# Latent attention on one core: the residual turned before it is scaled, wider compressed projections, four banks for the fills, and the keys squared on GpSimd

## The chip, the cores and the metric

One core of one Trainium2 chip runs the whole program. The metric is the device time of one execution in microseconds (us), as the median of several runs. Lower is better. All of the times below are of this core. The engines are named as in the profile: PE is TensorE's matmul side and PEld its weight load, DVE is VectorE, ACT is ScalarE, POOL is GpSimd, SP is SyncE, which issues most DMAs.

## What is computed

Two blocks of a transformer run on a sequence of 512 positions with a residual of 1024 columns. The first block has a gated mixer and dilated attention and a feed-forward layer with a norm behind it. The second block has two layers: layer 0 mixes with latent attention (the stage of this study) and layer 1 with an mLSTM, each followed by a feed-forward layer with a squared ReLU. The part that matters, from the reference:

```python
def mla_mixer(h, w_dq, q_norm, w_uq, w_dkv, kv_norm, w_ukv, q_gain, k_gain, w_o):
    b, s, _ = h.shape
    pos = jnp.arange(s)
    cq = rms_norm_2(h @ w_dq, q_norm)
    q = (cq @ w_uq).reshape(b, s, MLA_HEADS, MLA_QK)
    dkv = h @ w_dkv
    ckv = rms_norm_2(dkv[..., :MLA_KV_RANK], kv_norm)
    k_rope = jnp.broadcast_to(dkv[..., None, MLA_KV_RANK:], (b, s, MLA_HEADS, MLA_ROPE))
    kv = (ckv @ w_ukv).reshape(b, s, MLA_HEADS, MLA_NOPE + MLA_V)
    k = jnp.concatenate([kv[..., :MLA_NOPE], k_rope], axis=-1)
    v = kv[..., MLA_NOPE:]
    q = rms_norm_2(q, q_gain)
    k = rms_norm_2(k, k_gain)
    ...
```

Here `h` is the residual x after `rms_norm_2(x, norm_mix[0])`, which is x divided by the root of its mean square plus 1e-6, times a gain for each column. The query rank is 384, the key and value rank 256, the shared rotary part 32 columns; there are 16 heads of 96 (64 plus 32 rotary) with values of 64.

## The kernel before

Every float32 product is made as three matmuls of a reduced float32 form (`mm3`, L82 to L84): each operand is split into a high part and the rest, the low part. ScalarE makes the high part of a unit of weights (`split_hi`, L320), VectorE subtracts it to get the low part (`split_lo`, L326). Weights come in units of at most 2048 columns of the buffers `raw_weights`, `weights_hi` and `weights_lo`, which hold two units each; `plan_units` lists them in the order of use, and SyncE loads them in that order (`load_unit`, L312). A split may overwrite the unit two before it once `release` says that enough groups of matmuls have ended; `held` adds groups of the next unit to that number.

Each engine runs its own list of instructions in the order written; semaphores tie them together. A function such as `ffn`, `mla_down` or `mla` writes the lists for one stage.

**The hand-over.** The feed-forward layer of the first block (`ffn`) ends with a norm over its output, and adds it to the residual X (`updated`, L1592), first for the row tiles 0 and 1, then for 2 and 3. The next norm (`norm_halves`, here with `whole=True`) goes by the same halves. ScalarE sums the squares of each tile (`last_sum`, L392) and takes the root (L397); VectorE inverts the roots and scales the rows into a buffer XN (`normed`, L432 and L436; ScalarE scales tile 3, `normed_last`, L441); TensorE transposes XN (`turned`, L451) into PSUM; ScalarE makes the high part with the gain (`hi`, L461), VectorE the low part (`lo`, L493). GpSimd takes part of the multiplications by the gain in the norm behind the feed-forward layer (L1350).

**The compressed projections** (`mla_down`). The first unit has 256 of the 384 query columns, the second the other 128 and the 32 shared rotary columns, the third the 256 key and value columns. For each row tile, TensorE runs `first` (8 steps of k, 256 columns) and `second` (8 steps, 160 columns) into one bank, tiles 0 and 1 before tiles 2 and 3, with the turning of the second half between them. Then come the key and value columns, four tiles. Each result is squared and summed on ScalarE (L1723, L1712) and normed on VectorE (L1744 to L1762).

**Latent attention** (`mla`). The 16 heads are in four groups g of four. For each group, TensorE fills queries (`q`, 384 columns) and keys with values (`kv`, 512 columns) for each of 4 row tiles; ScalarE empties each bank (`empty`, L1952 to L1965). The jobs take the banks 5 and 7 in turn, and a job waits until the one before it in its bank is emptied. ScalarE squares the queries and the keys of a group into one buffer SQ (`squares`, L1975), VectorE sums them (`sums`, L2054), rotates (`rotate`, L2074 to L2077) and scales the keys (`norm`). Groups 0 and 1 are filled ahead of the heads, groups 2 and 3 among them. For each head n: scores (L1889), mask and maximum on VectorE (`mask`, L2086, and `shift`, L2093), exponentials on ScalarE (L1986), transposes of the probabilities in three parts (`turn`, L1899), copies to SBUF (parts 0 and 2 on ScalarE, L2032; part 1 on VectorE, L2153), values (L1911). The weights of later groups are split between heads, as `SPLITS` says: head 1 splits unit 4, which is the third query unit.

## Time and profile before

| What | Before |
|---|---|
| median of 3 runs | 2036.82 us (2035.33 to 2037.03) |
| the profiled execution | 2034.55 us |
| its span, first to last instruction | 2032.8 us |
| PE busy | 2010.8 us (99%) |
| DVE, ACT, POOL busy | 942.5, 844.7, 22.0 us |
| hand-over and compressed projections | about 837 to 887 us of the span |
| latent attention | about 887 to 1060 us |

An instruction's row in the timeline has its start, its duration, engine and line, what it writes and reads, and the count where neighbours of a kind are merged. What stands in brackets at the end is the time for which the engine was idle before it, and what ended that. Matmuls are pipelined, so the duration of one is longer than the distance between two starts; the distance is what a stream of them costs. Line numbers are those of the kernel before.

### The profile page before, as it was taken

The numbers are of one execution on the slowest core, as the hardware profiler recorded it, in microseconds if no ns is written. First come the engines' busy times: TensorE is split into PE (matmuls) and PEld (weight loads), VectorE is DVE, ScalarE is ACT, GpSimd is POOL, SyncE is SP. The second block draws the span as 40 slices with busy tenths as digits, with TensorE's granted clock in tenths as the row PEclk, the third lists the DMA queues.
The fourth block names the chain that finished last, engine by engine and source line by source line (L and its number), as shares of the span: only waits on it lengthen the run. The fifth ranks groups of instructions, "written<-read, shape, count | busy, mean of one in ns | idle before, by whom it ended". The sixth has DMA issues, their size and how long they took to land.

```text
span 2032.8 us, 24823 instructions
## 1 busy us (share of the span) xinstructions
PE 2010.8 (99%) x10074; PEld 1699.7 (84%) x10074; DVE 942.5 (46%) x1328; ACT 844.7 (42%) x1181; POOL 22.0 (1%) x38
## 2 busy tenths in 40 slices
PE   8999999999999999999999999999999999999999
PEld 7888888888888888887889888888888789888887
DVE  5654553345434343656745443434433455343443
ACT  5333324225433333558854433333464544333332
POOL 1000000000000000010000000000000000000000
PEclk9999999999999999999999999999999999999999
DMA  7232222332233323211012332232222123323322
GB/s 235 80 86 73 78 75 67 102 114 94 86 101 103 99 87 103 66 57 44 21 43 84 104 103 96 89 103 86 81 83 82 64 63 103 104 83 103 100 91 81
DMA packets 162880, 178.84 MB, mean 88 GB/s; under 512 B 7001, under 2 KB 125358, under 8 KB 162674
## 3 DMA queue, kind: packets, MB, share of 16 engines
q1 hardware_dynamic: 161762, 176.62, 27.4%
q8 instruction: 57, 0.93, 0.2%
q0 software_dynamic: 1024, 1.12, 0.2%
q14 instruction: 21, 0.17, 0.0%
q10 hardware_dynamic: 16, 0.00, 0.0%
HBM read 174.51 MB, written 2.10 MB: 87 GB/s over the span
## 4 chain that ended last, share of the span: by engine, by line
PE 93%; DVE 4%; ACT 2%; issue 0%; DMA 0%; SPq 0%; DVEq 0%; ACTq 0%
PE psum L82 28%; PE psum L83 28%; PE psum L84 28%; PE psum L1911 1%; PE psum L1889 1%; DVE weights_lo L326 1%; PE psum L842 1%; PE psum L2325 1%; PE psum L820 1%; PE psum L1899 1%; PE psum L451 1%; PE psum L1867 0%; PE psum L2308 0%; PE psum L828 0%; ACT weights_hi L320 0%
## 5 line engine op out<-in xcount | busy, mean ns | idle before, releaser
L82 PE MATMUL psum<-norm_T_hi,weights_hi 128*128 128x512 f32 (+1 forms) x1440 | 538.6, 374 | 0.7 <-DVE norm_T_lo L493 0.5
L84 PE MATMUL psum<-norm_T_hi,weights_lo 128*128 128x512 f32 (+1 forms) x1440 | 533.5, 370 | 0.0
L83 PE MATMUL psum<-norm_T_lo,weights_hi 128*128 128x512 f32 (+1 forms) x1440 | 533.1, 370 | 0.0
L82 PE MATMUL psum<-weights_hi,act_T_hi 128*128 128x512 f32 (+1 forms) x912 | 354.1, 388 | 2.3 <-DVE weights_lo L326 1.0
L84 PE MATMUL psum<-weights_hi,act_T_lo 128*128 128x512 f32 (+1 forms) x912 | 352.4, 386 | 0.0
L83 PE MATMUL psum<-weights_lo,act_T_hi 128*128 128x512 f32 (+1 forms) x912 | 352.3, 386 | 0.0
L1432 ACT ACTIVATE weights_hi<-raw_weights 128x2048 fp32r<-128x2048 f32 x92 | 175.7, 1910 | 343.7 <-PE psum L84 343.7
L82 PEld LDWEIGHTS psum<-norm_T_hi,weights_hi 128*128 128x128 f32 x1440 | 271.3, 188 | 46.8 <-DVE norm_T_lo L493 0.8
L84 PEld LDWEIGHTS psum<-norm_T_hi,weights_lo 128*128 128x128 f32 x1440 | 271.2, 188 | 46.6
L83 PEld LDWEIGHTS psum<-norm_T_lo,weights_hi 128*128 128x128 f32 x1440 | 271.5, 189 | 45.2
L1529 DVE TENSOR_TENSOR weights_lo<-raw_weights,weights_hi 128x2048 fp32r<-128x2048 f32 x92 | 210.9, 2292 | 110.4 <-ACT weights_hi L1432 110.4
L326 DVE TENSOR_TENSOR weights_lo<-raw_weights,weights_hi 128x2048 fp32r<-128x2048 f32 (+3 forms) x74 | 157.1, 2123 | 167.9 <-ACT weights_hi L320 167.9
L1537 DVE TENSOR_TENSOR act_T_lo<-scratch,act_T_hi 128x512 fp32r<-128x512 f32 x96 | 66.6, 694 | 318.3 <-ACT act_T_hi L1443 318.3
L82 PEld LDWEIGHTS psum<-weights_hi,act_T_hi 128*128 128x128 f32 x912 | 171.2, 188 | 37.6 <-issue 1.4
L84 PEld LDWEIGHTS psum<-weights_hi,act_T_lo 128*128 128x128 f32 x912 | 171.2, 188 | 33.6
L83 PEld LDWEIGHTS psum<-weights_lo,act_T_hi 128*128 128x128 f32 x912 | 171.3, 188 | 33.2
L1439 ACT ACTIVATE scratch<-psum 128x512 f32<-128x512 f32 x96 | 57.3, 597 | 273.5 <-PE psum L84 273.5
L320 ACT ACTIVATE weights_hi<-raw_weights 128x2048 fp32r<-128x2048 f32 (+3 forms) x74 | 130.9, 1769 | 71.7 <-PE psum L84 71.7
L82 PE MATMUL psum<-weights_hi,norm_T_hi 128*128 128x512 f32 (+3 forms) x384 | 134.7, 351 | 1.1 <-DVE norm_T_lo L493 0.9
L83 PE MATMUL psum<-weights_lo,norm_T_hi 128*128 128x512 f32 (+3 forms) x384 | 132.3, 345 | 0.0
L84 PE MATMUL psum<-weights_hi,norm_T_lo 128*128 128x512 f32 (+3 forms) x384 | 132.2, 344 | 0.0
L1546 DVE TENSOR_TENSOR residual<-psum,residual 128x512 f32<-128x512 f32 x112 | 76.5, 691 | 103.3 <-PE psum L84 103.3
(266 smaller groups left out, 1816.7 us busy)
## 6 DMA issues: line engine op xcount, KB each, us to landing
raw_weights<-in_ffn_w_dram SPq DMA_DIRECT2D x64, 1024.0 KB, 5.2
raw_weights<-in_w_up_dram SPq DMA_DIRECT2D x16, 1024.0 KB, 5.3
raw_weights<-in_w_down_dram SPq DMA_DIRECT2D x16, 1024.0 KB, 5.1
raw_weights<-in_w_in_dram SPq DMA_DIRECT2D x26, 512.0 KB, 5.1
raw_weights<-in_w_in_dram SPq DMA_DIRECT2D x11, 1024.0 KB, 5.2
raw_weights<-in_mlstm_w_in_dram SPq DMA_DIRECT2D x8, 1024.0 KB, 5.1
raw_weights<-in_w_in_dram SPq DMA_DIRECT2D x24, 256.0 KB, 3.4
raw_weights<-in_w_out_dram SPq DMA_DIRECT2D x4, 1024.0 KB, 5.1
```

The lines of the kernel that those rows point to most:

```text
L82: pe.matmul(out, ah, bh, start=start, stop=False)
L83: pe.matmul(out, ah, bl, start=False, stop=False)
L84: return pe.matmul(out, al, bh, start=False, stop=stop)
L320: act.activation(WH[:, u % 2, 0:c], RAW[:, u % 2, 0:c], ACT.Copy).then_inc(w_hi, 1)
L326: dve.tensor_tensor(WL[:, u % 2, 0:c], RAW[:, u % 2, 0:c], WH[:, u % 2, 0:c].bitcast(F32), SUB).then_inc(w_lo, 1)
L451: mm = pe.transpose(PS[:, bank, q * P:q * P + P], XN[:, t, k * P:k * P + P], IDENT[:, :])
L820: mm = pe.matmul(at_bank, QK[:, h % 2, g, 0, t * P:t * P + P], QK[:, h % 2, g, 1, lo * P:hi * P], start=True, stop=True)
L1432: act.activation(WH[:, u % 2, :], RAW[:, u % 2, :], ACT.Copy).then_inc(w_hi, 1)
L1439: act.activation(HS[:, f, :], PS[:, up_banks[f], :], ACT.Relu).then_inc(fr.sem, 1)
L1529: dve.tensor_tensor(WL[:, u % 2, :], RAW[:, u % 2, :], WH[:, u % 2, :].bitcast(F32), SUB).then_inc(w_lo, 1)
L1537: dve.tensor_tensor(AL[:, f, :], HS[:, f, :], AH[:, f, :].bitcast(F32), SUB).then_inc(fl.sem, 1)
L1546: dve.tensor_tensor(z, PS[:, banks[t], :], z, ADD).then_inc(acc.sem, 1)
```

## The change

Five things change, all in this part of the program.

1. `norm_halves` gets a form `behind=True`, used for the norm ahead of latent attention. TensorE turns X itself, as soon as its tiles are updated. The rows aren't scaled. The sums of squares (`row_sum`), roots and factors are made later. The compressed query and key norms take the missing factor into account: with r the mean square plus 1e-6 of a row, the epsilon inside their mean becomes r times 1e-6, and the common factor cancels. The shared rotary columns are multiplied by the factor when they are copied.
2. The first two units are cut along k instead of along columns: each has four steps of k with all 416 columns (384 query and 32 rotary), so that one matmul covers 416 columns.
3. The jobs up to the first heads (the first 20) go over four banks, 5, 7, 4 and 6.
4. GpSimd squares the keys of groups 1 to 3.
5. Unit 4 is split ahead of the heads (on ScalarE behind the first key tile of group 1, on VectorE ahead of the first mask), and VectorE sums and rotates group 1's queries ahead of the first mask.

```diff
-    add(4, dq[:, :, 0:256], held=2)
-    add(4, dq[:, :, 256:384], dkv[:, :, 256:288], side=True)
+    for i in range(2):
+        add(4, dq[:, 4 * i:4 * i + 4, :], dkv[:, 4 * i:4 * i + 4, 256:288], side=True, held=0 if i else 2)
...
                 def turned(pe, h):
-                    pe.wait_ge(xnc.sem, xnc.at(3 if whole and h else 2 * h + 2))
-                    if whole and h:
-                        pe.wait_ge(xlc.sem, xlc.at(1))
+                    if behind:
+                        pe.wait_ge(updated.sem, updated.at(2 * h + 2))
+                    else:
+                        pe.wait_ge(xnc.sem, xnc.at(3 if whole and h else 2 * h + 2))
+                        if whole and h:
+                            pe.wait_ge(xlc.sem, xlc.at(1))
...
# ffn, ScalarE
-                    for t in (0, 1):
-                        act.wait_ge(res.sem, res.at(t + 1))
-                        nxt.last_sum(act, t)
                     split_hi(act, u0 + 4 * NF)
# ffn, VectorE
                     updated(0)
-                    nxt.normed(dve, 0)
                     add(0, 2)
...
# mla_down, TensorE
+                def rows(i, t, ready=None):
+                    tt = slice(t * P, t * P + P)
+                    for k in range(4 * i, 4 * i + 4):
+                        if ready:
+                            ready(pe, k)
+                        w = slice(416 * (k % 4), 416 * (k % 4) + 416)
+                        mm = mm3(pe, PS[:, banks[t], 0:416], NTH[:, k, tt], NTL[:, k, tt],
+                                 WH[:, (u0 + i) % 2, w], WL[:, (u0 + i) % 2, w], k == 0, k == KD - 1)
+                    mm.then_inc(gemm, 1)
                 pe.wait_ge(w_lo, u0 + 1)
-                first(0)
-                first(1)
+                rows(0, 0, norm.ready(0))
+                rows(0, 1)
                 pe.wait_ge(w_lo, u0 + 2)
-                second(0)
-                second(1)
+                rows(1, 0, norm.ready(0))
+                rows(1, 1)
                 norm.turned(pe, 1)
-                first(2)
-                first(3)
-                second(2)
-                second(3)
+                rows(0, 2, norm.ready(1))
+                rows(0, 3)
+                rows(1, 2, norm.ready(1))
+                rows(1, 3)
# mla_down, ScalarE
+                for t in (0, 1):
+                    norm.row_sum(act, t)
+                norm.hi(act, 1)
                 for t in (2, 3):
                     act.wait_ge(res_in.sem, res_in.at(t + 1))
-                    norm.last_sum(act, t)
-                norm.normed_last(act)
-                norm.hi(act, 1)
+                    norm.row_sum(act, t)
+                norm.row_roots(act)
                 split_hi(act, u0 + 2)
# mla_down, VectorE
-                norm.normed(dve, 1)
                 norm.lo(dve, 1)
+                norm.row_means(dve)
+                norm.row_factors(dve)
                 split_lo(dve, u0 + 2)
                 dve.wait_ge(sq.sem, sq.at(4))
-                dve.tensor_scalar(m0[:, 0:4], s0[:, 0:4], 1.0 / QR, EPS, MUL, ADD).then_inc(ms.sem, 1)
+                dve.wait_ge(norm.means_made.sem, norm.means_made.at(2))
+                dve.wait_ge(norm.factor_made.sem, norm.factor_made.at(1))
+                dve.scalar_tensor_tensor(m0[:, 0:4], s0[:, 0:4], 1.0 / QR, norm.eps, MUL, ADD).then_inc(ms.sem, 1)
...
-                    dve.tensor_copy(KRR[:, t, :], PS[:, banks[t], QR:QR + MROPE]).then_inc(kr_c.sem, 1)
+                    dve.tensor_scalar(KRR[:, t, :], PS[:, banks[t], QR:QR + MROPE], norm.factor[:, t:t + 1], None, MUL).then_inc(kr_c.sem, 1)
...
# mla
             def bank(m):
-                return 5 if m % 2 == 0 else 7
-            SPLITS = {1: 4, 2: 5, 3: 6, 5: 7, 10: 8, 13: 9}
+                return (5, 7, 4, 6)[m % 4] if m < 20 else (5, 7)[m % 2]
+            SPLITS = {2: 5, 3: 6, 5: 7, 10: 8, 13: 9}
...
# mla, ScalarE
                 for t in range(NT):
                     empty(("kv", 1, t))
+                    if t == 0:
+                        split_hi(act, u0 + 4)
...
-                    if n % 4 == 0 and g < 4:
-                        squares(g, 1)
# mla, GpSimd
+            @block.gpsimd
+            def _(pool):
+                for g in range(1, 4):
+                    pool.wait_ge(xn.sem, xn.at(g + 1))
+                    pool.wait_ge(ms.sem, ms.at(3 * g + 1))
+                    pool.wait_ge(ev.sem, ev.at(emptied[idx[("kv", g, NT - 1)]]))
+                    k = QKB[:, g % 2, 1536:3072]
+                    pool.tensor_tensor(SQ, k, k, MUL).then_inc(sq.sem, 1)
# mla, VectorE
                 norm(0)
+                sums(1, 0)
+                rotate(1, 0)
+                split_lo(dve, u0 + 4)
                 mask(0, 3)
                 shift(0, slice(3, 4))
                 masks(0)
-                sums(1, 0)
-                rotate(1, 0)
...
-            after = norm_halves(C_N0, *turn[1], halves, whole=True)
+            after = norm_halves(C_N0, *turn[1], halves, behind=True)
```

The new steps of the norm:

```python
def row_sum(act, t):
    act.activation(XN[:, t, :], X[:, t, :], ACT.Square, accum_out=s1[:, t:t + 1]).then_inc(s1c.sem, 1)
def row_roots(act):
    act.wait_ge(m0c.sem, m0c.at(1))
    act.activation(root, m0, ACT.Sqrt).then_inc(rtc.sem, 1)
def row_means(dve):
    dve.wait_ge(s1c.sem, s1c.at(NT))
    dve.tensor_scalar(m0, s1, 1.0 / D, EPS, MUL, ADD).then_inc(m0c.sem, 1)
    dve.wait_ge(m0c.sem, m0c.at(1))
    dve.tensor_scalar(s0, m0, EPS, None, MUL).then_inc(m0c.sem, 1)
def row_factors(dve):
    dve.wait_ge(rtc.sem, rtc.at(1))
    dve.reciprocal(rstd, root).then_inc(rsc.sem, 1)
```

## Rows read from the trace of the kernel before

**Rows 1.** Windows: busy time (count) of PE, PEld, DVE, ACT, POOL; granted clock; DMA.

```profile
600.00:800.00 200.00, 200.00 (x885) 165.58 (x884) 79.72 (x75) 66.86 (x72) 0.00 (x0) 1.00 0.31 100
...
924.00:936.00 12.00, 10.09 (x72) 8.80 (x73) 11.69 (x36) 11.41 (x19) 0.00 (x0) 1.00 0.00 1
```

**Rows 2.** Waits of TensorE, 840 to 1030 us: total, times, longest.

```profile
PE psum L82 <- ACT scratch L1952: 0.7, 2, 0.4
...
PE psum L82 <- ACT scratch L1958: 0.6, 1, 0.6
```

**Rows 3.** Timeline of TensorE, 842 to 863 us, the hand-over.

```profile
842.99 1.97 PE L451 MATMUL psum<-ident,scratch 128*128 128x128 f32 x16 [1.13 <-DVE scratch L436]
...
848.03 0.36 PE L82 MATMUL psum<-weights_hi,norm_T_hi 128*128 128x256 f32 x1 [0.35 <-DVE norm_T_lo L493]
...
860.26 1.94 PE L451 MATMUL psum<-ident,scratch 128*128 128x128 f32 x16 [0.78 <-ACT scratch L441]
...
862.73 0.39 PE L82 MATMUL psum<-weights_hi,norm_T_hi 128*128 128x256 f32 x1 [0.53 <-DVE norm_T_lo L493]
```

**Rows 4.** Timeline of TensorE, 924 to 936 us, the first heads.

```profile
924.25 0.41 PE L1899 MATMUL psum<-ident,scratch 128*128 128x128 f32 x2 [0.88 <-ACT scratch L2032]
...
931.64 0.41 PE L1899 MATMUL psum<-ident,scratch 128*128 128x128 f32 x2 [0.49 <-ACT scratch L2032]
...
935.28 0.41 PE L82 MATMUL psum<-weights_hi,act_T_hi 128*128 128x384 f32 x1 [1.03 <-DVE weights_lo L326]
```

**Rows 5.** Timeline of TensorE: starts of one kind, of 256, 160 and 384 columns.

```profile
852.91 0.28 PE L82 MATMUL psum<-weights_hi,norm_T_hi 128*128 128x256 f32 x1
...
853.63 0.28 PE L82 MATMUL psum<-weights_hi,norm_T_hi 128*128 128x256 f32 x1
...
855.63 0.27 PE L82 MATMUL psum<-weights_hi,norm_T_hi 128*128 128x160 f32 x1
...
856.30 0.28 PE L82 MATMUL psum<-weights_hi,norm_T_hi 128*128 128x160 f32 x1
...
892.36 0.33 PE L82 MATMUL psum<-weights_hi,act_T_hi 128*128 128x384 f32 x1
...
892.88 0.33 PE L82 MATMUL psum<-weights_hi,act_T_hi 128*128 128x384 f32 x1
```

**Rows 6.** Timeline of VectorE and ScalarE, 837 to 873 us.

```profile
837.11 2.48 DVE L1592 SCALAR_TENSOR_TENSOR residual<-scratch,small,residual 128x1024 f32<-128x1024 f32 x2
...
851.63 1.28 DVE L1575 TENSOR_TENSOR scratch<-psum,scratch 128x512 f32<-128x512 f32 x2
...
854.57 2.48 DVE L1592 SCALAR_TENSOR_TENSOR residual<-scratch,small,residual 128x1024 f32<-128x1024 f32 x2
...
869.04 1.92 ACT L320 ACTIVATE weights_hi<-raw_weights 128x2048 fp32r<-128x2048 f32 x1 [5.09 <-PE psum L84]
...
870.99 2.29 DVE L326 TENSOR_TENSOR weights_lo<-raw_weights,weights_hi 128x2048 fp32r<-128x2048 f32 x1 [5.96 <-ACT weights_hi L320]
```

**Rows 7.** Timeline of VectorE: the split beside GpSimd's multiplications.

```profile
844.04 3.06 DVE L326 TENSOR_TENSOR weights_lo<-raw_weights,weights_hi 128x2048 fp32r<-128x2048 f32 x1
```

**Rows 8.** Timeline of VectorE and ScalarE, 918 to 964 us.

```profile
918.20 0.69 DVE L2086 CUSTOM_DVE_ANT_0 scratch<-psum,chunk_masks 128x512 f32<-128x512 f32 x1 [7.86 <-PE psum L1889]
...
920.30 1.75 DVE L2054 TENSOR_REDUCE small<-scratch 128x16 f32<-128x1536 f32 x1
...
924.09 0.68 DVE L2086 CUSTOM_DVE_ANT_0 scratch<-psum,chunk_masks 128x512 f32<-128x512 f32 x1
...
961.28 1.48 ACT L1975 ACTIVATE scratch<-scratch 128x1536 f32<-128x1536 f32 x1
...
963.11 0.60 ACT L2032 ACTIVATE scratch<-psum 128x512 f32<-128x512 f32 x1 [0.34 <-PE psum L1899]
...
963.95 0.16 DVE L2093 SCALAR_TENSOR_TENSOR small<-small 128x1 f32<-128x1 f32 x1
```

**Rows 9.** Source line L1350: ns minimum, median, maximum; first and last start us.

```profile
L1350 POOL TENSOR_TENSOR scratch<-scratch x2: 1271/2302/3332, 843.7 to 844.9; 128x512 f32<-128x512 f32 x2
```

More of the change, by code:

```diff
@@ L370, in in_order, with norm_halves @@
             return x.rearrange("p (i r) -> p r i", r=NT)
-        def norm_halves(which, banks_a, banks_b, part, whole=False, apart=False):
+        def norm_halves(which, banks_a, banks_b, part, whole=False, apart=False, behind=False):
             XN = SCR[:, 0:NT * D].rearrange("p (t d) -> p t d", t=NT)
@@ L377, in norm_halves @@
             marks = {}
-            for c, n in ((n_s0, 0 if whole or apart else NT), (n_s1, 3 if apart else NT), (n_sv, 1 if apart else 0), (n_m0, 0 if whole or apart else 2),
-                         (n_rt, 3 if apart else NT), (n_rs, 3 if apart else 2), (n_xn, 3 if whole else NT), (n_xl, 1 if whole else 0), (n_tp, 8), (n_th, 2 * KD), (n_tl, 2 * KD)):
+            updated = resid.copy()
+            for c, n in ((n_s0, 0 if whole or apart or behind else NT), (n_s1, 3 if apart else NT), (n_sv, 1 if apart else 0), (n_m0, 2 if behind else 0 if whole or apart else 2),
+                         (n_rt, 1 if behind else 3 if apart else NT), (n_rs, 1 if behind else 3 if apart else 2), (n_xn, 0 if behind else 3 if whole else NT), (n_xl, 1 if whole else 0), (n_tp, 8), (n_th, 2 * KD), (n_tl, 2 * KD)):
                 marks[c] = c.copy()
@@ L450, in turned @@
                             k, t = 2 * b + q // 2, 2 * h + q % 2
-                            mm = pe.transpose(PS[:, bank, q * P:q * P + P], XN[:, t, k * P:k * P + P], IDENT[:, :])
+                            mm = pe.transpose(PS[:, bank, q * P:q * P + P], (X if behind else XN)[:, t, k * P:k * P + P], IDENT[:, :])
                         mm.then_inc(tpc.sem, 1)
@@ L502, in ready @@
                     return wait
+            Steps.eps, Steps.factor, Steps.means_made, Steps.factor_made = s0, rstd, m0c, rsc
             return Steps
@@ L1678, in _ @@
             def _(pe):
-                def first(t):
-                    group_N(pe, u0, 0, 256, 256, KD, PS[:, banks[t], 0:256], t, NTH, NTL,
-                            ready=None if t % 2 else norm.ready(t // 2))
-                def second(t):
-                    group_N(pe, u0 + 1, 0, 160, 160, KD, PS[:, banks[t], 256:416], t, NTH, NTL)
+                def rows(i, t, ready=None):
[7 more added lines that the diff above has]
+                    mm.then_inc(gemm, 1)
                 pe.wait_ge(w_lo, u0 + 1)
-                first(0)
-                first(1)
+                rows(0, 0, norm.ready(0))
+                rows(0, 1)
                 pe.wait_ge(w_lo, u0 + 2)
-                second(0)
-                second(1)
+                rows(1, 0, norm.ready(0))
+                rows(1, 1)
                 norm.turned(pe, 1)
-                first(2)
-                first(3)
-                second(2)
-                second(3)
+                rows(0, 2, norm.ready(1))
+                rows(0, 3)
+                rows(1, 2, norm.ready(1))
+                rows(1, 3)
                 pe.wait_ge(w_lo, u0 + 3)
@@ L1756, in _ @@
                 dve.wait_ge(sq.sem, sq.at(8))
-                dve.tensor_scalar(m0[:, 4:8], s0[:, 4:8], 1.0 / KVR, EPS, MUL, ADD).then_inc(ms.sem, 1)
+                dve.scalar_tensor_tensor(m0[:, 4:8], s0[:, 4:8], 1.0 / KVR, norm.eps, MUL, ADD).then_inc(ms.sem, 1)
                 dve.wait_ge(rt.sem, rt.at(2))
@@ L1845, in job @@
                     m = idx[what]
-                    if m >= 2:
-                        pe.wait_ge(ev.sem, ev.at(emptied[m - 2]))
-                        if order[m - 2][0] == "out":
-                            pe.wait_ge(tl.sem, tl.at(order[m - 2][1] + 1))
+                    same = [i for i in range(m) if bank(i) == bank(m)]
+                    if same:
+                        last = same[-1]
+                        pe.wait_ge(ev.sem, ev.at(emptied[last]))
+                        if order[last][0] == "out":
+                            pe.wait_ge(tl.sem, tl.at(order[last][1] + 1))
                     kind = what[0]
```

5 lines of the change are left out of this document (added).

## The prediction

> **What bounds the kernel now.** I read the windows first, because a share of busy time over the whole span hides where the losses lie. In a stretch of feed-forward work TensorE has no idle time, 200.00 of 200.00 us; from 924 to 936 us it was busy for 10.09 of 12.00 us, while VectorE was busy for 11.69 and ScalarE for 11.41 [rows 1]. So TensorE sets the end nearly everywhere, and a stage is worth changing in two ways only: its idle time, or its own work. The profile's engine shares (the table above) say the same: 99% for TensorE, so all its idle time together is 22 us.
>
> Next the waits of TensorE between 840 and 1030 us: a few tenths each, for instance 0.7 us in two waits on the copies that empty the query products and 0.6 us in one on those of the keys and values [rows 2]. Then the timeline of TensorE. In the hand-over from the feed-forward layer to the compressed projections it idles 1.13 and 0.35 us around the first turning of the residual, 0.78 and 0.53 us around the second [rows 3]. Among the heads of latent attention it idles 0.88 and 0.49 us for the ScalarE copy on L2032 and 1.03 us for the low part of weights [rows 4]. The clock column shows full speed (1.00, the 2.4 GHz level) in both windows [rows 1]; nothing here changes what precedes it, so it stays out of the sum.
>
> **Part 1: 416 columns in one matmul.** Before, each of 4 row tiles took 8 x 3 products of 256 columns and 8 x 3 of 160: 96 of each. After, 96 of 416. Starts of the same kind six matmuls apart (three for 384 columns) give the pitch: 256 columns (853.63 - 852.91) / 6 = 0.120 us; 160 columns (856.30 - 855.63) / 6 = 0.112 us; 384 columns (892.88 - 892.36) / 3 = 0.173 us [rows 5]. The 160-column matmul costs almost what the 256-column one does: there is a floor. From 256 to 384 columns the slope is 0.053 / 128, so 416 columns should take 0.173 + 32 x 0.00042 = 0.187 us. Saving: 96 x (0.120 + 0.112 - 0.187) = 4.3 us, all of it on TensorE's own path. Bounds: no less than the 384-column pitch (saving 5.6), no more than that of 512 columns, 200 / 885 = 0.226 us [rows 1] (saving 0.6). I take 0.187, since 416 lies next to 384.
>
> The Trainium skill (TensorE: Matmul & The Clock Gate, section Back-to-back issue gap) gives N / 2.4 + 2.5 ns for an isolated matmul. By it 256 and 160 columns cost 109 + 69 ns and 416 costs 176 ns, so joining them saves an estimated 0.2 us in all: it speaks against this part, and would put the whole change at 3.7 us instead of 7.8. The trace disagrees with it, with 112 ns at 160 columns [rows 5].
>
> **Part 2: the residual turned unscaled, first half.** The turning waited for the sum of squares, the root, the reciprocal and the scaling. Now it waits only for the update of the residual, which ended at 837.11 + 2.48 = 839.6 us [rows 6], before TensorE was free at 842.99 - 1.13 = 841.9 [rows 3]. The 1.13 us go. The 0.35 us behind them came from VectorE reaching the low parts late (848.03): it stood behind the scaling and behind one weight split that took 3.06 us [rows 7]. The scaling leaves this queue and the split covers 1664 columns instead of 2048, so it goes too. With the restart of the pipe (0.1 to 0.2 us each) I take 1.7 us; bounds 1.1 and 1.8.
>
> **Part 3: the second half.** TensorE reaches it after 48 wide matmuls: 848.03 - 1.7 + 48 x 0.187 = 855.3 us. Before, the update ended 5.4 us after VectorE's additions of 851.63 (854.57 + 2.48 = 857.05) [rows 6]. These stand behind the second weight split, and all of that chain moves up by what the first half gained, about 1.7 us, less 0.4 us because the second split grows from 1280 to 1664 columns and plus 0.2 us that its ScalarE part waited. Additions at 850.1, update ended at 855.5, turning at 855.6: 0.3 us idle instead of 0.78. The 0.53 us from the turning to the first product stay, as that is ScalarE and VectorE making the first high and low parts. After it VectorE delivers a pair of tiles each 0.8 us, and TensorE now needs 6 x 0.187 = 1.1 us for a pair, so the small pacing losses that the second half showed (some 0.3 us) go. I take 0.8 us; bounds 0 and 1.2. The sums of squares move to ScalarE's spare time behind the high parts; their factors are wanted only by the norms of the compressed tiles, later.
>
> What becomes late next is the third unit's split. It can start when two of the four second-half groups are done: before at 869.04, low part ready at 870.99 + 2.29 = 873.3 [rows 6], and TensorE came 1.1 us later. Now half of the remaining work is 24 x 0.187 = 4.5 us, while high and low parts take 1.9 + 2.3 us and the hand-overs: they meet within 0.1 us. I charge nothing and keep 0.5 us for the range. The new multiplications by the factor replace instructions of the same size; the unit loads have the same total bytes and are issued earlier. Sum for the projections: 4.3 + 1.7 + 0.8 = 6.8 us.
>
> **Part 4: four banks and the moved split.** From here VectorE is nearly the path: it is busy nearly without a pause from 924 to 936 us [rows 1], but it idled 7.86 us before the first mask at 918.20 [rows 8]. The four banks let TensorE run further ahead in the fills, so their waits [rows 2], some 2 us with restarts, go, and the first scores are there near 914.5. In its freed time, from 918.20 - 7.86 = 910.3, VectorE now does the sums and rotation of group 1's queries (920.30 to 924.09, 3.8 us) [rows 8] and the split that TensorE waited for (1152 columns, by 2.29 us for 2048 some 1.4 us) [rows 6]. If nothing else came, the first mask would be at 910.3 + 3.8 + 1.4 = 915.5 instead of 918.2. The transposes followed it by 924.25 - 918.20 = 6.05 us, 0.88 of it for ScalarE's square [rows 4], which leaves; I keep 0.8 us for ScalarE's other copies, which then press, and get 921.5 instead of 924.25. The waits of 0.49 and 1.03 us, with their restarts 1.85 us, also go: ScalarE no longer splits that unit between heads, and its low part is made. Gain 2.75 + 1.85 = 4.6 us.
>
> **Part 5: GpSimd squares the keys.** A multiply of 128x512 on GpSimd took between 1.27 and 3.33 us [rows 9]; in the same stretch VectorE's weight split lasted 3.06 us instead of 2.29 [rows 6, 7]. I read this as turns: VectorE stood until the first multiply ended, GpSimd stood until the split ended. The square has 1536 columns: 3 x 1.27 = 3.8 us if it has its turn; 3 x 3.33 = 10 us is the other bound. I assume that VectorE instructions that read PSUM are free of it, as only the split was long, and that every one with two SBUF operands is not. The Trainium skill (GPSIMD Engine Reference, Specifications) says the SBUF interfaces are shared with VectorE, with contention for instructions with two SBUF inputs. The trace agrees, with 3.06 against 2.29 us.
>
> Group 1: the square can start when group 1's keys are out and its query sums are read, about 912.7, in the middle of the rotation and ahead of the split. If VectorE stands 3.8 us there, the first mask comes at 919.3 and the transposes at 919.3 + 6.05 - 0.88 = 924.5: part 4's 2.75 us are lost and 1.6 us remain. If VectorE keeps the port until the split is done, only its small shift instruction waits, and some 3.2 us remain. Groups 2 and 3: the square starts where ScalarE's did, 961.28, and ends at about 965.1. In it falls the shift at 963.95, a two-SBUF operation: it waits some 1 us, and the copy behind it, which TensorE waits for, too. ScalarE gains nothing there, for it sat idle 0.34 us after its square anyway [rows 8]. I take 0.7 us lost in each; bounds 0 and 1.1. Sum for attention: 2.4 (midway between 1.6 and 3.2, as no row says who has the turn) - 1.4 = 1.0 us.
>
> **The number.** 6.8 + 1.0 = 7.8 us. The profiled execution took 2034.55 us (span 2032.8), 2.3 us under the median of 2036.82; I set the gain against its own terms, giving 2026.7, and against the median 2029.0 us.
>
> **Rivals.**
> (a) GpSimd is in nobody's way: VectorE's long split was long for another reason. For it: the two durations on GpSimd differ by a factor of 2.6, a sign that one is odd. Against it: the times fit turns. Gain 6.8 + 4.6 = 11.4: 2025.4 us.
> (b) The wide matmul costs the sum of the narrow ones: gain 7.8 - 4.3 = 3.5 us, 2033.3 us. The rows at 160 and 384 columns speak against it. This is where the rule named in part 1 would lead.
> (c) The third unit's weights come late: nearer 2 us than 0.1 us, from ScalarE still at sums and root when the split is due. 2030.9 us. Against it: those end a microsecond before it.
> (d) The change does not do what it says at the hand-over: the update of the residual, not the norm, is last, and the idle times stay. Gain 7.8 - 2.5 = 5.3: 2031.5 us. For it: in the second half the update is indeed within 0.3 us of last.
> (e) Slower. Each square takes the 10 us of the second multiply and VectorE's two-operand work stands for it. Group 1 loses 6.2 us more; in groups 2 and 3 the sums, due at 966.7, come at 971.3, 4.6 us each. 6.8 + 1.6 - 6.2 - 9.2 = -7.0 us: 2043.8 us. Beyond 5.4 us all three squares count, and it decides from about 7.7 us a square: (d - 3.8) + 2 x (d - 5.4) = 8.4.
>
> **Chances.** Forecast 0.55, (a) 0.22, (b) 0.06, (c) 0.07, (d) 0.05, (e) 0.05. A measurement of this kernel tells about 0.2%, 4.1 us, from no change. Faster: forecast, (a), (c), (d), 0.89; within it (b), 0.06; slower (e), 0.05. Range: below, (a) with its own microsecond of scatter, 2024.0; above, the forecast with part 1 at 0.2 us and 1.1 us lost per square, through (c) and (d), 2032.5.
>
> **What would show it.** 96 matmuls of 128x416 at a pitch near 0.187 us; no idle time before the first transposes of L451 and 0.2 to 0.4 us before the second; squares on GpSimd of 3.8 us; in the same stretch a rotation or split on VectorE two or three times its usual length; shifts of 1 us in groups 2 and 3; no wait on low weights at the second query group. Wrong would be a pitch over 0.2 us, a square over 7 us, or a new wait on low weights before the third unit.

## The result, and the profile after

The changed kernel takes 2026.03 us (median of 4 runs, 2024.82 to 2027.68), the kernel before 2036.74 us (4 runs, 2035.33 to 2037.03). The ratio is 0.995, with a 95% interval of 0.9938 to 0.9962: 10.7 us faster. The profiled execution after took 2025.99 us (span 2024.2), against 2034.55 us before: 8.6 us between the two traces. The 2.1 us between these two gains go with the granted clock of the runs of before, which is taken up below. The four runs of the changed kernel differ in it too: the one with a mean clock of 1.000 took 2024.82 us, two with 0.999 took 2025.99 and 2026.07, and one with 0.998 took 2027.68.

The page's line of engines after:

```profile
PE 2006.0 (99%) x9978; PEld 1695.8 (84%) x9978; DVE 943.2 (47%) x1326; ACT 837.4 (41%) x1174; POOL 30.5 (2%) x41
```

TensorE's busy time fell by only 4.8 us (2010.8 to 2006.0), so about half of the gain is idle time. The waits of TensorE after, 836 to 1030 us (line waited on, total, times, longest):

```profile
PE psum L1925 <- DVE small L2131: 2.2, 1, 2.2
PE psum L82 <- DVE norm_T_lo L521: 0.5, 1, 0.5
PE psum L1947 <- DVE scratch L2199: 0.4, 1, 0.4
PE psum L1935 <- ACT scratch L2068: 0.4, 2, 0.2
```

The waits on ScalarE in the fills [rows 2] and the one on the low weights [rows 4] are gone, of those on ScalarE's copies among the heads 0.4 us are left, and one new wait of 2.2 us has come: the scores of the second head, on the masks that VectorE makes of the first (L2131).

**The projections.** TensorE after, from the turning of the residual (L479) through the compression (416 columns) to the first query product (384 columns):

```profile
841.81 0.40 PE L84 MATMUL psum<-weights_hi,act_T_lo 128*128 128x512 f32 x1
842.04 1.91 PE L479 MATMUL psum<-ident,residual 128*128 128x128 f32 x16
843.71 0.47 PE L82 MATMUL psum<-weights_hi,act_T_hi 128*128 128x512 f32 x1
...
850.49 0.36 PE L82 MATMUL psum<-weights_hi,norm_T_hi 128*128 128x416 f32 x1
...
851.62 0.36 PE L82 MATMUL psum<-weights_hi,norm_T_hi 128*128 128x416 f32 x1
...
855.38 0.34 PE L84 MATMUL psum<-weights_hi,norm_T_lo 128*128 128x416 f32 x1
855.73 1.97 PE L479 MATMUL psum<-ident,residual 128*128 128x128 f32 x16
858.22 0.46 PE L82 MATMUL psum<-weights_hi,norm_T_hi 128*128 128x416 f32 x1 [0.53 <-DVE norm_T_lo L521]
...
880.34 0.34 PE L82 MATMUL psum<-weights_hi,act_T_hi 128*128 128x384 f32 x1
```

The turnings carry no bracket any more, where before they stood behind 1.13 and 0.78 us of idle time [rows 3]. The second starts 0.35 us after the last matmul where the pitch is 0.19: 0.16 us lost. The 0.53 us behind it stayed. Six wide matmuls take 851.62 - 850.49 = 1.13 us: a pitch of 0.188 us. The first query product starts at 880.34 instead of 886.95, 6.61 us earlier; the last product of the feed-forward layer started 0.34 us later than before (841.81, against 841.47 in the trace of before), so the projections themselves gained 6.95 us.

**The first heads.** TensorE after. L1925 makes scores, L1935 turns the masked scores, L1947 multiplies them with the values, and the last line is the second group's first query product:

```profile
911.97 3.79 PE L1925 MATMUL psum<-key_rows,scratch 96*128 96x512 f32 x8 [2.25 <-DVE small L2131]
915.56 0.92 PE L1935 MATMUL psum<-ident,scratch 128*128 128x128 f32 x4
916.32 0.60 PE L1903 MATMUL psum<-ident,scratch 128*96 128x128 f32 x4
...
917.63 0.38 PE L1935 MATMUL psum<-ident,scratch 128*128 128x128 f32 x2
...
920.03 2.38 PE L1925 MATMUL psum<-key_rows,scratch 96*128 96x512 f32 x8
...
926.60 0.42 PE L82 MATMUL psum<-weights_hi,act_T_hi 128*128 128x384 f32 x1
```

The last line answers to 935.28 [rows 4]: 8.68 us earlier, of which 6.61 were already there, so the attention added 2.07 us. Behind the wait of 2.25 us the same eight score matmuls took 3.79 us, and 2.38 us one head later. The windows (length, busy time and count of TensorE, granted clock, DMA share, GB/s) say why:

```profile
908.00:910.00 2.00, 1.72 (x7) 1.00 0.00 0
910.00:912.00 2.00, 0.03 (x1) 1.00 0.00 0
912.00:914.00 2.00, 2.00 (x4) 0.70 0.50 163
914.00:916.00 2.00, 2.00 (x8) 0.50 0.38 140
916.00:918.00 2.00, 2.00 (x19) 0.95 0.00 0
```

The granted clock fell to 0.50, the 1.2 GHz level, right behind the idle time, and was back at 2.4 GHz some 4 us later. It cost 3.79 - 2.38 = 1.4 us in the scores, and some 0.3 us more in the four transposes behind them, which took 916.32 - 915.56 = 0.76 us from start to start (0.44 in e5 below). VectorE in the same stretch, with the rotation (L2119 to L2122), the split (L327), the first mask (L2131) and the shift (L2138):

```profile
905.43 1.29 DVE L2119 TENSOR_TENSOR scratch<-scratch 128x512 f32<-128x512 f32 x2
906.76 2.85 DVE L2121 TENSOR_TENSOR scratch<-scratch 128x256 f32<-128x256 f32 x1
909.54 0.41 DVE L2122 TENSOR_TENSOR scratch<-scratch 128x256 f32<-128x256 f32 x1
909.87 1.34 DVE L327 TENSOR_TENSOR weights_lo<-raw_weights,weights_hi 128x1152 fp32r<-128x1152 f32 x1
911.14 0.68 DVE L2131 CUSTOM_DVE_ANT_0 scratch<-psum,chunk_masks 128x512 f32<-128x512 f32 x1
```

And GpSimd's three squares (L2088):

```profile
906.28 3.05 POOL L2088 TENSOR_TENSOR scratch<-scratch 128x1536 f32<-128x1536 f32 x1 [22.45 <-ACT scratch L1994]
952.69 2.75 POOL L2088 TENSOR_TENSOR scratch<-scratch 128x1536 f32<-128x1536 f32 x1 [43.35 <-ACT scratch L1994]
991.37 2.75 POOL L2088 TENSOR_TENSOR scratch<-scratch 128x1536 f32<-128x1536 f32 x1 [35.93 <-ACT scratch L1994]
```

The rotation of 256 columns took 2.85 us where its twin took 0.41: it ended 0.3 us after the first square did (906.28 + 3.05 = 909.33). VectorE stood for 2.4 us, the first mask was made that much later, and TensorE ran dry.

### The profile page after: what moved, and what is told of

Read it like the earlier page. It is cut to its first block, busy times and chain, and to the rows that moved or that the text cites. A ratio compares the mean times of both kernels' runs of the same rounds, so it can differ in the third digit from the quotient of the medians.

```text
span 2024.2 us, 24613 instructions
## 1 busy us (share of the span) xinstructions
PE 2006.0 (99%) x9978; PEld 1695.8 (84%) x9978; DVE 943.2 (47%) x1326; ACT 837.4 (41%) x1174; POOL 30.5 (2%) x41
## 4 chain that ended last, share of the span: by engine, by line
PE 94%; DVE 3%; ACT 1%; DMA 0%; issue 0%; SPq 0%; ACTq 0%; DVEq 0%
PE psum L82 28%; PE psum L84 28%; PE psum L83 28%; PE psum L1947 2%; PE psum L1925 2%; PE psum L871 1%; PE psum L2371 1%; PE psum L849 1%; PE psum L1935 1%; PE psum L479 1%; DVE weights_lo L327 1%; PE psum L1903 1%; PE psum L2354 0%; PE psum L857 0%; ACT weights_hi L321 0%; DMA raw_weights<-in_w_in_dram 0%
## 5 line engine op out<-in xcount | busy, mean ns | idle before, releaser
L327 DVE TENSOR_TENSOR weights_lo<-raw_weights,weights_hi 128x2048 fp32r<-128x2048 f32 (+3 forms) x74 | 156.9, 2121 | 166.7 <-ACT weights_hi L321 166.6
L82 PE MATMUL psum<-weights_hi,norm_T_hi 128*128 128x512 f32 (+3 forms) x352 | 127.6, 362 | 1.1 <-DVE norm_T_lo L521 0.5
L84 PE MATMUL psum<-weights_hi,norm_T_lo 128*128 128x512 f32 (+3 forms) x352 | 125.5, 357 | 0.0
L83 PE MATMUL psum<-weights_lo,norm_T_hi 128*128 128x512 f32 (+3 forms) x352 | 125.4, 356 | 0.0
```

What stands on the lines that cost most here:

```text
L82: pe.matmul(out, ah, bh, start=start, stop=False)
L83: pe.matmul(out, ah, bl, start=False, stop=False)
L84: return pe.matmul(out, al, bh, start=False, stop=stop)
L327: dve.tensor_tensor(WL[:, u % 2, 0:c], RAW[:, u % 2, 0:c], WH[:, u % 2, 0:c].bitcast(F32), SUB).then_inc(w_lo, 1)
```

## The experiments

Each kernel ran on one of three chips, beside runs of the kernel before on the same chip; their medians there were 2035.08 (e1 to e4), 2036.78 (e5 to e8) and 2036.88 us (e9, e10), of 19, 9 and 9 runs. The chips themselves are alike: the runs of before with a mean clock of 1.000 took 2034.79 to 2035.31, 2034.97, and 2034.80 and 2034.85 us on them. Edits are against the changed kernel where nothing else is said.

**e1: narrow units again.** The compression has units of 256 and 160 columns and its loops as before; the norm and the attention stay as changed.

```
-    for i in range(2):
-        add(4, dq[:, 4 * i:4 * i + 4, :], dkv[:, 4 * i:4 * i + 4, 256:288], side=True, held=0 if i else 2)
+    add(4, dq[:, :, 0:256], held=2)
+    add(4, dq[:, :, 256:384], dkv[:, :, 256:288], side=True)
...
```

> The changed kernel with the units of before: 256 and 160 columns in two matmuls instead of 416 in one. Theory: the pitch decides, 96 x (0.120 + 0.112 - 0.187) = 4.3 us come back; about 0.3 us of it may be hidden, since the update of the residual is no longer waited for in the second half. Span about 2028.2 instead of 2024.2 us. Rival: streaming of columns alone sets the cost (0.2 us by the rule named in the prediction), and the gain at the projections came from the earlier turning; then the span stays within 0.5 us of 2024.2.

Measured: 2029.84 us (ratio 0.9973, 0.9962 to 0.9983), span 2027.9, 3.7 us over that of the changed kernel, and the first query product at 884.08, 3.74 us later. The wide rows are worth 3.7 us behind the new norm, where 4.3 less some 0.3 were expected, and the wait of 2.2 us before the scores is there as well.

**e2: the norm as before, wide rows kept.** The residual is scaled before it is turned.

```
-                halves, behind=True)
+                halves, whole=True)
...
                     updated(0)
+                    nxt.normed(dve, 0)
```

> The changed kernel with the norm of before at the hand-over (rows scaled ahead of the turning), wide matmuls and the new attention kept. Theory: TensorE idles again about 1.1 and 0.35 us around the first turning, and around the second more than the 0.78 us of before, since the wide matmuls bring it there 2.2 us earlier while the chain sum of squares, root, scaling still takes 3.2 us behind the update: some 3.3 us idle in place of 0.2. Span about 2024.2 + 1.7 + 3.1 = 2029 us. Rival: each part stands alone, and undoing this one costs the 2.5 us that the prediction gave it: 2026.7 us.

Measured: 2031.38 us (ratio 0.9979, 0.997 to 0.9988), span 2030.1: 5.9 us over, where 4.8 were expected and 2.5 by the rival. The second turning in it, and TensorE's windows there:

```profile
860.84 3.24 PE L479 MATMUL psum<-ident,scratch 128*128 128x128 f32 x16 [3.31 <-ACT scratch L466]
863.74 0.70 PE L82 MATMUL psum<-weights_hi,norm_T_hi 128*128 128x416 f32 x1
```

```profile
860.00:862.00 2.00, 1.16 (x8) 0.82 0.00 0
862.00:864.00 2.00, 2.00 (x11) 0.50 0.00 0
864.00:866.00 2.00, 2.00 (x11) 0.82 0.00 0
```

The wait was 0.78 us [rows 3] and is 3.31 us: the wide rows bring TensorE to the second half sooner, and the scaled tiles come no sooner. Then the clock falls, and from the first transpose to the next product are 863.74 - 860.84 = 2.90 us instead of 843.71 - 842.04 = 1.67. These 1.2 us are about what the expectation lacked. The time from the last product of the feed-forward layer to the first query product gives all four pairings of norm and rows:

| Norm | Rows | from, to | us |
|---|---|---|---|
| old | narrow (before) | 841.47, 886.95 | 45.48 |
| old | wide (e2) | 842.06, 886.29 | 44.23 |
| new | narrow (e1) | 841.58, 884.08 | 42.50 |
| new | wide (the change) | 841.81, 880.34 | 38.53 |

With the old norm the wide rows are worth 1.25 us and with the new one 3.97: with the old one, most of what they save goes into a wait that is 2.5 us longer and into the fall of the clock behind it. So the two parts can't be priced apart and added (3.7 + 5.9 is more than the 6.95 us of both).

**e3: the attention as before.** Two banks, the old split, the squares on ScalarE; the function of the latent attention is that of before, all else is the changed kernel. The core of the edit:

```
-                return (5, 7, 4, 6)[m % 4] if m < 20 else (5, 7)[m % 2]
+                return 5 if m % 2 == 0 else 7
-            SPLITS = {2: 5, 3: 6, 5: 7, 10: 8, 13: 9}
+            SPLITS = {1: 4, 2: 5, 3: 6, 5: 7, 10: 8, 13: 9}
...
+                    if n % 4 == 0 and g < 4:
+                        squares(g, 1)
```

> The changed kernel with the whole attention stage of before (two banks, keys squared by ScalarE, unit 4 split at head 1), new hand-over and projections kept. Theory: the stage gained 2.1 us in the trace (935.28 to 926.60 is 8.7 us, 6.6 of them already there at its first query product), so the span is about 2026.3 us. Rival: the stage's gain is only the position of one trace, and the span stays within 0.5 us of 2024.2.

Measured: 2029.37 us (ratio 0.9968, 0.9955 to 0.998), span 2027.5: 3.3 us over, 1.2 more than expected. The expectation set a trace with a fall of the clock (the change) against one without (before); here both have one. At a mean clock of 1.000 the difference is the same: 2028.0 us in two runs against 2024.8 in one. TensorE has its old waits back, and the clock falls behind the last of them (the columns as above):

```profile
917.39 0.41 PE L1932 MATMUL psum<-ident,scratch 128*128 128x128 f32 x2 [0.88 <-ACT scratch L2065]
924.79 0.41 PE L1932 MATMUL psum<-ident,scratch 128*128 128x128 f32 x2 [0.50 <-ACT scratch L2065]
928.43 0.54 PE L82 MATMUL psum<-weights_hi,act_T_hi 128*128 128x384 f32 x1 [1.03 <-DVE weights_lo L327]
```

```profile
928.00:930.00 2.00, 1.57 (x5) 0.64 0.20 27
930.00:932.00 2.00, 2.00 (x8) 0.51 0.72 268
```

These are the waits of [rows 4], and in the trace of before the clock stayed at 1.00 behind them. So the same three waits are followed by a fall in one execution and by none in another; two of the six runs of e3 have a mean clock of 1.000. What decides it, no run here shows.

**e4: the first square later.** GpSimd squares the second group's keys only when the first head's masks are made.

```
                 for g in range(1, 4):
+                    if g == 1:
+                        pool.wait_ge(smk.sem, smk.at(4))
                     pool.wait_ge(xn.sem, xn.at(g + 1))
```

> The changed kernel, in which GpSimd's first square waits until VectorE has made the masks of head 0, when VectorE idles 3.4 us. Theory (turns on the SBUF port): the rotation instruction that took 2.85 us takes 0.42 again, the first mask comes 2.4 us earlier, TensorE's 2.25 us wait for it goes, and the span falls by some 2.3 us to about 2021.9. Rival 1: the rotation was long for a reason of its own, and nothing changes. Rival 2: the wait goes to another link (exponentials, or the copies on ScalarE) and less than 1 us is gained.

Measured: 2021.80 us (2021.67 to 2022.06, 5 runs; ratio 0.9932, 0.9918 to 0.9945), span 2020.1: 4.1 us less than the changed kernel, where 2.3 were expected, and the clock is at 1.0 in every run. VectorE and GpSimd in it:

```profile
906.75 0.42 DVE L2123 TENSOR_TENSOR scratch<-scratch 128x256 f32<-128x256 f32 x1
...
908.70 0.68 DVE L2133 CUSTOM_DVE_ANT_0 scratch<-psum,chunk_masks 128x512 f32<-128x512 f32 x1
```

```profile
910.71 2.74 POOL L2090 TENSOR_TENSOR scratch<-scratch 128x1536 f32<-128x1536 f32 x1 [26.87 <-DVE small L2133]
```

The square lasts 2.74 us, as in the other groups, but lies where VectorE is idle or reads PSUM, but for a shift of one column just ahead of its end (913.25, 0.21 us for 0.16). The rotation is back at 0.42 us, the first mask comes 2.44 us earlier, and neither the wait nor the fall of the clock is there. This is the fastest kernel of the study, faster than both given ones.

**e5: TensorE kept busy in the wait.** Nine matmuls of 512 columns into a bank that is free at that time, ahead of the second head's scores; their product is thrown away.

```
+                        if n == 1 and i == 0:
+                            for r in range(9):
+                                pe.matmul(PS[:, 7, :], AH[:, r % 3, 0:P], AL[:, r % 3, :], start=True, stop=True)
                         if n and c == 0:
                             pe.wait_ge(smk.sem, smk.at(4 * n - 4 + (1, 3, 4)[b]))
```

> The changed kernel with nine matmuls of 512 columns, whose result nobody reads, put where TensorE waits 2.25 us for the first mask. The wait itself stays. Theory: the wait costs twice, once as idle time and once because the granted clock falls to 0.5 behind it (the scores at 911.97 took 3.79 us instead of 2.38). With TensorE busy the clock stays at 1.00 and the span falls by 1.4 us to about 2022.8, and the spread of the runs shrinks. Rival: the fall has nothing to do with the idle time; then the span stays at 2024.2 or grows by what the nine matmuls overlap.

Measured: 2024.32 us (2024.12 to 2024.86, 5 runs; ratio 0.994, 0.9926 to 0.9953), span 2022.5: 1.7 us less by doing more.

```profile
909.55 2.41 PE L1925 MATMUL psum<-act_T_lo,act_T_hi 128*128 128x512 f32 x9
912.01 2.45 PE L1928 MATMUL psum<-key_rows,scratch 96*128 96x512 f32 x8
914.30 0.60 PE L1938 MATMUL psum<-ident,scratch 128*128 128x128 f32 x4
914.74 0.60 PE L1903 MATMUL psum<-ident,scratch 128*96 128x128 f32 x4
```

The scores start where they did (912.01 against 911.97) and take 2.45 us instead of 3.79. So the 1.4 us are the clock's and not the scores' own. The four transposes behind them are back at 0.44 us from start to start, and the second group's query product starts at 925.02 for 926.60: the fall cost 1.6 us in all, which is what the span shows (1.7). The DMA traffic behind the wait isn't the cause: from 912 to 916 us the DMA share in e5 is 0.47 and 0.39, as in the change (0.50 and 0.38), at a clock of 1.00. All five runs have a mean clock of 1.000. Of the twelve runs of the change and of e1, whose traces have the same wait, three do: the idle time makes the fall likely, and not certain.

**e6: the squares by ScalarE.** The changed kernel with GpSimd's block taken out and ScalarE squaring the keys between heads, as before; four banks and the moved split stay.

```
                         split_hi(act, u0 + SPLITS[n])
+                    if n % 4 == 0 and g < 4:
+                        squares(g, 1)
```

> The changed kernel without GpSimd's squares: ScalarE squares the keys of groups 1 to 3 as before. Theory: the long rotation is gone as in the late-square kernel, so most of its 4.1 us are gained too; ScalarE's 1.48 us ahead of the copies of head 0 cost up to 1 us of it: span 2020.1 to 2021.1. In groups 2 and 3 nothing changes. Rival: GpSimd's squares are what relieves ScalarE, and without them all heads at 0, 4 and 8 lose about 1 us each: 2023 us.

Measured: 2022.54 us (2022.45 to 2022.72; ratio 0.9931, 0.9917 to 0.9944), span 2020.7. That is 3.5 us less than the changed kernel and 0.6 us more than e4, as expected. GpSimd's help, as placed in the change, costs 3.5 us; placed as in e4 it is worth 0.6 us. The difference to e4 lies in this wait of e6, which is 0.4 us there:

```profile
PE psum L1935 <- ACT scratch L2070: 1.2, 3, 0.7
```

**e7: two banks.** The late square of e4, with two banks for the fills.

```
-                return (5, 7, 4, 6)[m % 4] if m < 20 else (5, 7)[m % 2]
+                return (5, 7)[m % 2]
```

> The late-square kernel (span 2020.1) with the fills back in two banks. Theory: the fills end later, about where they did in the kernel with the attention of before (first scores near 910.3 instead of 907.3 us), so the first mask comes some 2.3 us later: span about 2022.4. Rival: VectorE's chain sets the first mask with either number of banks, and the four banks are worth less than 0.5 us.

Measured: 2025.24 us (ratio 0.9944, 0.993 to 0.9958), span 2023.2: 3.1 us over e4, where 2.3 were expected. The first mask is at 911.65, 2.95 us later than in e4. The waits of the fills are back (0.7 us in two on the query copies, 0.6, 0.3 and 0.2 us on those of keys and values), so the four banks are worth 3.1 us beside the late square.

**e8: the other squares under a shift.** The late square, and those of the third and fourth group start behind the first mask of the second head of the group in work, so that the shift of 128x3 falls into them. This edit is against e4.

```
-                    if g == 1:
-                        pool.wait_ge(smk.sem, smk.at(4))
+                    pool.wait_ge(smk.sem, smk.at(4 if g == 1 else 4 * (4 * g - 3) + 1))
```

> The late-square kernel, in which GpSimd's squares of groups 2 and 3 also start late, when the first mask of head 5 or 9 is made, so that the second shift (three columns, two SBUF operands) and three masks (PSUM and SBUF operands) fall into them. Theory of the prediction: every instruction with two SBUF operands stands until the square ends; the shift waits some 1 us, and the span grows by 1 to 2 us to about 2021.6. Rival: such small instructions don't stand; masks and shifts keep their 0.16 to 0.69 us and the span stays at 2020.1.

Measured: 2022.53 us (2022.38 to 2025.69; ratio 0.9936, 0.9923 to 0.995), span 2020.6: 0.5 us over e4, between the two expectations. The median may hide a second cost: two of the five runs have a mean clock of 0.998 and 0.999 and took 2025.69 and 2024.14 us, the other three 2022.38 to 2022.53, and e4 has no such run. Where those two fell was not traced. GpSimd and VectorE:

```profile
951.16 2.75 POOL L2089 TENSOR_TENSOR scratch<-scratch 128x1536 f32<-128x1536 f32 x1 [37.83 <-DVE small L2132]
```

```profile
951.19 0.69 DVE L2200 COPY scratch<-psum 128x512 f32<-128x512 f32 x1
951.80 0.55 DVE L2132 CUSTOM_DVE_ANT_0 scratch<-psum,chunk_masks 128x384 f32<-128x384 f32 x1
...
952.95 0.98 DVE L2139 SCALAR_TENSOR_TENSOR small<-small 128x3 f32<-128x3 f32 x1
```

Inside the square the copy and the mask, which read PSUM, keep their times (0.69 and 0.55 us). The shift, three columns with two operands in SBUF, takes 0.98 us instead of 0.16: it ends when the square has ended, at 951.16 + 2.75 = 953.91. The same happens in the fourth group (992.19, 0.98 us). The turns are thus real, and they cover even so small an instruction.

**e9: the split moved back.** The late square, with the third query split beside the first head again, as before.

```
-            SPLITS = {2: 5, 3: 6, 5: 7, 10: 8, 13: 9}
+            SPLITS = {1: 4, 2: 5, 3: 6, 5: 7, 10: 8, 13: 9}
```

> The kernel after with GpSimd's square of the second group of keys held until the first head's masks are made, and the third query split back at its old place beside the first head. Against the same kernel with the split moved (span 2020.1 us), my theory: ScalarE makes the hi half (1.16 us) and VectorE the lo half (1.3 us) between the first head's passes instead of ahead of them, where both are on the way to the second head; the first head's masks are not later, the second head's lose 0.5 to 1.3 us: span 2021.0. Rival: there is room beside the first head as GpSimd no longer stands there, so nothing changes (2020.1), or the split gains since it leaves the way to the first mask, 2019.

Measured: 2022.87 us (2022.74 to 2023.08; ratio 0.9934, 0.992 to 0.9947), span 2021.3: 1.2 us over e4, near the expected 0.9. The second group's query product in it:

```profile
923.75 0.41 PE L82 MATMUL psum<-weights_hi,act_T_hi 128*128 128x384 f32 x1 [0.84 <-DVE weights_lo L327]
```

This is the wait of 1.03 us of [rows 4] again, and 0.24 us of a ScalarE copy ahead of it: the moved split is worth 1.2 us. It costs nothing at its new place (the first mask is at 908.55 here and at 908.70 in e4).

**e10: narrow units with the late square.** As e1, on top of e4.

> The same late square, with the units of the compression of 256 and 160 columns as before instead of two of 416. Both kernels should be free of falls of the clock, so this is the price of the wide rows alone: my theory 3.7 us (span 2023.8, 32 fewer products of 160 columns at 0.112 us against 0.0 and those of 256 and 416 at their own rates), as it was with the square early. Rival: part of the 3.7 us was an accident of the clock or of what stands behind, and it is below 3 us (span under 2023.1).

Measured: 2025.66 us (2025.64 to 2025.93; ratio 0.9948, 0.9935 to 0.9962), span 2023.9: 3.8 us over e4. With no fall of the clock in either kernel, the price of e1 stands.

## Why the prediction was right, and where its terms were off

The likeliest case came out: faster, by its mechanisms, within the range. The forecast was a gain of 7.8 us in the profiled execution and 8.6 were measured there; the 2029.0 us set against the median came out at 2026.03. That the first pair is so close is in part luck. At a mean clock of 1.000 on both sides the change gains 10.1 us (2034.9 - 2024.8), and in the attention, where 1.0 us was forecast and 2.07 were measured, three errors offset each other: part 4 gave 6.1 us for 4.6, the squares held VectorE for 2.5 us where they were charged with 3.6, and the clock took 1.6 us that were charged with nothing. The upper end of the range doesn't come out of its own terms either: 2029.0 + 4.1 + 0.8 is 2033.9 with a saving of 0.2 us in part 1, and 2031.0 with a pitch of 0.2 us, not 2032.5; the measured time is far from all of them.

**Part 1 (4.3 us).** Right. The pitch is 0.188 us for 0.187, and e1 and e10 give 3.7 and 3.8 us. Rival (b) is gone. The rule for an isolated matmul in the Trainium skill (TensorE: Matmul & The Clock Gate, section Back-to-back issue gap), by which joining the matmuls would save an estimated 0.2 us, doesn't hold for these streams: the traces disagree with it, by the 3.7 us of e1 and 0.112 us at 160 columns [rows 5].

**Parts 2 and 3 (1.7 and 0.8 us).** Right. No idle time before the first turning, 0.16 us before the second for the forecast 0.3, the 0.53 us behind it unchanged, and no wait on the third unit. With part 1 the sum was 6.8 and is 6.95 us; rivals (c) and (d) are gone. What the prediction didn't see is how the parts hang together (e2): at the old norm the wide rows are worth 1.25 us.

**Part 4 (4.6 us).** Too small. In e4, where nothing is in its way, the second group's query product starts at 922.54: 935.28 - 922.54 - 6.61 = 6.1 us gained. The first mask was forecast for 915.5, which is 908.9 once the 6.61 us are taken off, and came at 908.70. The term that was off is the way from it to the transposes: 0.8 us were kept for ScalarE's other copies, and no such wait came (913.52 - 908.70 = 4.8 us, where 6.0 were forecast). e7 and e9 give the four banks 3.1 us and the moved split 1.2. The sums and the rotation moved ahead of the first mask weren't undone by themselves, so their share is not shown.

**Part 5 (a loss of 3.6 us).** Its total was near by luck, and its pieces were wrong. The squares took 4.1 us away (e4 against the change). The prediction had 2.2 us of it in group 1, between its bounds of 1.4 and 3.0, and 1.4 us in groups 2 and 3. Measured at the second group's query product, group 1 lost 2.5 us by VectorE's standing (925.02 in e5 against 922.54 in e4) and 1.6 us by the clock (926.60 against 925.02), and groups 2 and 3 lost nothing: from the first mask of head 5 to that of head 9 are 38.67 us in the kernel before (963.22 to 1001.89), where ScalarE squares, and 38.68 in the change (954.57 to 993.25). The term that was off is the duration of a square, which stands on 3 x 1.27 = 3.8 us. It was 2.75 us. With 1.27 us at 512 columns [rows 9] and 2.75 at 1536, the slope is 1.45 ns a column and some 0.5 us are there once for each instruction, and these had been counted three times. A square of 2.75 us from 952.69 ends at 955.44, when the shift is due (955.30, 0.16 us, not lengthened); one of 3.8 us would have held it. The mechanism itself is shown by e4 and e8, so rival (a) is false although its time, 2025.4 us, lies nearer to the median measured than the forecast's. Rival (e) is gone with the duration.

The Trainium skill (SBUF — State Buffer, section Who interferes with whom) says that a VectorE instruction with two SBUF inputs contends with a GpSimd instruction that reads SBUF, and that one with at most one SBUF input, outside the modes that use both ports, doesn't. It calls the shared pair of ports an exclusive lock and says, of those modes, that whichever engine issues first has the pair for its whole instruction. The traces agree, and show the turns by whole instructions for two SBUF inputs too: 2.85 against 0.41 us and 0.98 against 0.16 us for two SBUF operands, 0.55 and 0.69 us, unchanged, for masks and copies out of PSUM.

**The clock.** "Nothing here changes what precedes it, so it stays out of the sum": this sentence is the step that failed. The wait that the change made brought a fall that cost 1.6 us (e5). The clock also accounts for the distance between the gains of the traces and of the medians. Of the 37 runs of the kernel before on the three chips, 15 had a mean granted clock of 1.000 and took 2034.8 to 2035.3 us, and 22 had 0.998 or 0.999 and took 2036.2 to 2037.4 us. The profiled one, with 2034.55 us and 1.000, was of the first kind; the median of 2036.74 us, which three of its four runs lie near, is of the second. Where in the program those 22 fell was not traced; e3 shows one place where it happens, behind the 1.03 us on the low weights. The change took away the waits of before and brought one of its own. The longest waits of TensorE in this stretch in e4, e6, e7, e9 and e10 are 0.5 to 0.8 us (in e9 the one of 0.84 us on the low weights), and all of their 25 runs are at 1.000, within 0.5 us of each other in each kernel. Against runs of before at the same clock, e4 gains 13.1 us (2034.9 - 2021.8).

## What to carry to other kernels

Give a two-operand job to GpSimd only where VectorE's next work reads PSUM or is idle: it is the start of the job, and not its length, that made a loss of 3.5 us out of a gain of 0.6. Where an engine gets faster, look what comes up behind it: the wide rows pay 4.0 us instead of 1.25 because the norm left the way of the second turning. For an instruction of unseen size take a slope and a fixed part from two sizes, not a multiple of one; and count a wait of TensorE of the sizes seen here (1.03 to 3.31 us) as the wait and a possible fall of the clock behind it, which makes the same program differ by 2 us from run to run.

## What the runs showed of the hardware that was not expected

- Idle times of TensorE of 2.25 us (the change) and 3.31 us (e2) in an otherwise unbroken stream were followed by some 4 us with a granted clock down to 0.50, the 1.2 GHz level, with losses of 1.6 us, and of 1.2 us in the sixteen transposes alone. With the same idle time filled by nine useless matmuls the clock stayed at the 2.4 GHz level and the kernel was 1.7 us faster. The fall isn't certain: three of the twelve runs of the change and of e1 have a mean clock of 1.000. Three waits of 0.88, 0.50 and 1.03 us within 11 us were followed by a fall in one traced execution (e3) and by none in another (before).
- A VectorE instruction of 3 columns stood 0.8 us behind a GpSimd multiply, until the multiply ended (0.98 us for 0.16).
- A GpSimd multiply of 128x1536 with itself took 2.75 us beside a VectorE that read PSUM, and 3.05 us where it had started inside a two-operand instruction of VectorE (906.28, in the pair that ended near 906.7).
